# Feature-product inputs in cells of a 128-row block by a token tile, placed 0 or 32 bytes into the cell by stage, with the low parts of the input weight chunks 32 bytes into their slots

## What is computed

```
h = rms_norm(x, g)            # 256 tokens x 1024
a = h @ w_in                  # input product, 1024 -> 2 x 2816 in a feed-forward part
x = x + f(a) @ w_out          # output product, 2816 -> 1024 there, 1024 -> 1024 in a mixer
```

## Time and profile before

| | before |
|---|---|
| three executions | 2536.23, 2537.78, 2538.86 us |
| the profiled execution | 2536.61 us, its span 2534.8 us |
| TensorE's granted clock | 1.0 of full speed throughout (2.4 GHz) |
| busy: PE, PEld, DVE, ACT | 2518.7, 2223.5, 1769.4, 1395.5 us |
| share of PE in the chain that ended last | 95% |

### The profile page before, as it was taken

The page is one execution under the profiler, slowest core; times in us unless marked ns, Lnnn a source line. Parts: engine busy times, 40 slices in busy tenths (PEclk is TensorE's granted clock), DMA queues, the critical chain, the costliest instruction groups (busy, mean ns, idle before and its releaser), DMA issues.

```text
span 2534.8 us, 37208 instructions
## 1 busy us (share of the span) xinstructions
PE 2518.7 (99%) x15209; PEld 2223.5 (88%) x15209; DVE 1769.4 (70%) x2500; ACT 1395.5 (55%) x2078; POOL 150.6 (6%) x228
## 2 busy tenths in 40 slices
PE   9999999999999999999999999999999999999999
PEld 9999888998888988888888888888988888898887
DVE  7778567885775777757657775775777577567773
ACT  7766476664554555545555554554555455455553
POOL 2100011000000000000010000002010000010000
PEclk9999999999999999999999999999999999999999
DMA  7266552664665556556564655655456556563763
GB/s 224 98 178 211 173 166 84 189 194 166 208 196 197 181 162 194 189 187 197 185 221 147 204 192 187 195 187 196 153 166 201 188 180 205 184 207 125 216 189 127
DMA packets 543027, 459.47 MB, mean 181 GB/s; under 512 B 10634, under 2 KB 500058, under 8 KB 542858
## 3 DMA queue, kind: packets, MB, share of 16 engines
q1 hardware_dynamic: 537351, 441.52, 54.9%
q0 software_dynamic: 4656, 15.30, 1.7%
q10 hardware_dynamic: 851, 0.28, 0.0%
HBM read 455.97 MB, written 1.10 MB: 180 GB/s over the span
## 4 chain that ended last, share of the span: by engine, by line
PE 95%; DVE 3%; ACT 1%; DMA 1%; issue 0%; POOL 0%; DVEq 0%; POOLq 0%; ACTq 0%
PE ps L964 28%; PE ps L847 23%; PE ps L846 11%; PE ps L829 5%; PE ps L830 5%; PE ps L831 5%; PE ps L784 2%; PE ps L783 2%; PE ps L782 2%; PE ps L765 2%; PE ps L766 2%; PE ps L767 2%; PE ps L849 1%; PE ps L687 1%; DVE wlo L1956 1%; PE ps L1065 1%
## 5 line engine op out<-in xcount | busy, mean ns | idle before, releaser
L1956 DVE TENSOR_TENSOR wlo<-raw,whi 128x2048 fp32r<-128x2048 f32 (+1 forms) x419 | 956.7, 2287 | 363.2 <-ACT whi L1362 363.1
L1362 ACT ACTIVATE whi<-raw 128x2048 fp32r<-128x2048 f32 (+2 forms) x421 | 800.3, 1906 | 293.2 <-DMA raw<-in_ff_w_out 161.1
L847 PE MATMUL ps<-h,whi 128*128 128x512 f32 x2560 | 873.6, 393 | 0.0
L846 PE MATMUL ps<-h,wlo 128*128 128x256 f32 x2240 | 629.7, 281 | 0.0
L847 PEld LDWEIGHTS ps<-h,whi 128*128 128x128 f32 x2560 | 459.7, 188 | 81.5
L846 PEld LDWEIGHTS ps<-h,wlo 128*128 128x128 f32 x2240 | 421.9, 188 | 15.3
L1362 ACT ACTIVATE u<-ps 128x512 f32<-128x512 f32 x160 | 96.0, 600 | 397.4 <-PE ps L847 397.4
L964 PE MATMUL ps<-whi,hid_hi 128*128 128x512 f32 x880 | 291.3, 390 | 0.0
L964 PE MATMUL ps<-whi,hid_lo 128*128 128x512 f32 x880 | 290.7, 389 | 0.0
L964 PE MATMUL ps<-wlo,hid_hi 128*128 128x512 f32 x880 | 290.3, 389 | 0.0
L829 PE MATMUL ps<-h,whi 128*128 128x256 f32 x1024 | 288.1, 281 | 0.0
(11 more groups left out here) (337 smaller groups left out, 3285.9 us busy)
## 6 DMA issues: line engine op xcount, KB each, us to landing
raw<-in_ff_w_in SPq DMA_DIRECT2D x160, 1024.0 KB, 5.6
raw<-in_ff_w_out SPq DMA_DIRECT2D x88, 1024.0 KB, 4.8
raw<-in_ffn_w_in SPq DMA_DIRECT2D x40, 1024.0 KB, 5.6
raw<-in_a_w_qkv SPq DMA_DIRECT2D x24, 1024.0 KB, 5.0
raw<-in_ffn_w_out SPq DMA_DIRECT2D x22, 1024.0 KB, 4.8
raw<-in_w_in SPq DMA_DIRECT2D x18, 1024.0 KB, 6.2
raw<-in_ff_w_in SPq DMA_DIRECT2D x32, 512.0 KB, 4.4
raw<-in_c_w_qkv SPq DMA_DIRECT2D x12, 1024.0 KB, 5.0
```

The costliest lines, as they stand in the source:

```text
L846: e.matmul(out[:, 0:SEQ], lo, m.h[:, 0, k, :], start=False, stop=False, skip_group_check=True)
L847: ins = e.matmul(view(out, a=2), hi, m.h[:, :, k, :], start=(k == 0), stop=(k == KT - 1), skip_group_check=True)
L1362: return self.nc.scalar.activation(*a, **k)
L1956: self.e.tensor_tensor(chunk_view(m.wlo[:, slot, :], c), chunk_view(m.raw[:, slot, :], c), chunk_view(m.whi[:, slot, :], c).bitcast(F32), ...
```

## The change

The tile `h` gets a dimension more: 2 x 8 x 2 cells of 128 + 16 floats, one for a block and a token tile (576 bytes apart). A stage's input product writes and reads its 128 floats 8 floats (32 bytes) into the cell, a mixer's output product at offset 0. A stream of 256 tokens is now two rows of 128 with 64 bytes between them, one of 512 four such rows. The slots of `raw`/`wlo` get 16 floats more (8256 bytes instead of 8192), and the chunks of input products are put 8 floats in, by the DMA too; those of output products stay at offset 0, and `whi` stays as it was. The fillers around `h` go; `v_mla` moves into other tiles' unused ends. In `mix` of the second layer, ScalarE evicts the first token tile before the `split` instead of after it, waiting for that tile's reciprocal deviation alone. No instruction is added or taken away.

```diff
+H_AT = {"out": 0, "mix1": 8, "mix2": 8, "ffn1": 8, "swiglu": 8}
+PAD = 16
+LOW_IN = 8
+LOW_SWIGLU = 8
...
-        dst, src = dst_src(self.m.raw[:, c % SLOTS, :], b)
+        dst, src = dst_src(low(self.m.raw, c), b)
...
-                hi, lo = w_of(m.whi[:, c % SLOTS, :], f, k), w_of(m.wlo[:, c % SLOTS, :], f, k)
-                e.matmul(out, hi, m.h_hi[:, k, :], start=(k == 0), stop=False)
-                e.matmul(out, hi, m.h_lo[:, k, :], start=False, stop=False)
-                ins = e.matmul(out, lo, m.h_hi[:, k, :], start=False, stop=(k == KT - 1))
+                hi, lo = w_of(m.whi[:, c % SLOTS, :], f, k), w_of(low(m.wlo, c), f, k)
+                e.matmul(out, hi, self.inputs[:, 0, k, :, :], start=(k == 0), stop=False)
+                e.matmul(out, hi, self.inputs[:, 1, k, :, :], start=False, stop=False)
+                ins = e.matmul(out, lo, self.inputs[:, 0, k, :, :], start=False, stop=(k == KT - 1))
...
-                hi, lo = w_of(m.whi[:, c % SLOTS, :], f, k), w_of(m.wlo[:, c % SLOTS, :], f, k)
+                hi, lo = w_of(m.whi[:, c % SLOTS, :], f, k), w_of(low(m.wlo, c), f, k)
                 if k > 0:
-                    e.matmul(out[:, 0:SEQ], lo, m.h[:, 0, k, :], start=False, stop=False, skip_group_check=True)
-                ins = e.matmul(view(out, a=2), hi, m.h[:, :, k, :], start=(k == 0), stop=(k == KT - 1), skip_group_check=True)
+                    e.matmul(view(out[:, 0:SEQ], a=TT), lo, self.inputs[:, 0, k, :, :], start=False, stop=False, skip_group_check=True)
+                ins = e.matmul(out.rearrange("p (a t c) -> p a t c", a=2, t=TT), hi, self.inputs[:, :, k, :, :], start=(k == 0), stop=(k == KT - 1), skip_group_check=True)
...
-        self.blocks(OUT_ORDER[what], (self.m.h_hi, self.m.h_lo, 0), False)
+        self.blocks(OUT_ORDER[what], (self.m.out_hi, self.m.out_lo, 0), False)
...
-        if l > 0:
-            self.split(0, 0)
-        e.wait_ge(s.rstd, TT * self.rounds["norm"])
         if l == 0:
+            e.wait_ge(s.rstd, TT * self.rounds["norm"])
             keep(0)
             self.split(0, 0)
             keep(1)
         else:
             for t in range(TT):
+                e.wait_ge(s.rstd, TT * (self.rounds["norm"] - 1) + t + 1)
                 self.evict_head(t, proj, C_CQ, HEAD_WIDTH, ACT.Copy)
+                if t == 0:
+                    self.split(0, 0)
...
+def low_places():
+
+    out = []
+    for stage in PLAN:
+        n, rows = chunks_of(stage), 4 if stage[0] in ("mix1", "mix2") else FT // 2
+        out += [LOW_SWIGLU if stage[0] == "swiglu" else LOW_IN] * (n - rows) + [0] * rows
+    return out
+
+
+def low(a, c):
+
+    return a[:, c % SLOTS, LOW_AT[c]:LOW_AT[c] + CW]
...
-            [("raw", [P, SLOTS, CW])],
-            [("wlo", [P, SLOTS, CW], F32R)])
-        sb(ctx, "in_front_of_h", [P, 8])
-        m.h = sb(ctx, "h", [P, 2, KT, SEQ], F32R)
-        sb(ctx, "behind_h", [P, 120])
-        m.h_hi, m.h_lo = m.h[:, 0, :, :], m.h[:, 1, :, :]
+            [("raw", [P, SLOTS, CW + PAD])],
+            [("wlo", [P, SLOTS, CW + PAD], F32R)])
+        m.h = sb(ctx, "h", [P, 2, KT, TT, P + PAD], F32R)
+        m.h_at = lambda stage: m.h[:, :, :, :, H_AT[stage]:H_AT[stage] + P]
+        m.out_hi, m.out_lo = (m.h_at("out")[:, i, :, :, :] for i in range(2))
```

More of the change, by code:

```diff
@@ L725, in turn_rows, with take @@
         ins.then_inc(s.rows_turned, 1)
+    def take(self, stage):
+        self.inputs = self.m.h_at(stage)
     def begin_product(self):
@@ L756, in tokens_tile @@
         c = self.c0 + b
-        whi, wlo = (a[:, c % SLOTS, :].rearrange("p (k c) -> p k c", k=KT)[:, :, 0:w] for a in (m.whi, m.wlo))
+        whi, wlo = (a.rearrange("p (k c) -> p k c", k=KT)[:, :, 0:w] for a in (m.whi[:, c % SLOTS, :], low(m.wlo, c)))
         out = m.ps[:, self.bank(b), t * 256:t * 256 + w]
@@ L772, in pair_tile @@
         c = self.c0 + b
-        whi, wlo = (a[:, c % SLOTS, 0:PAIR * w].rearrange("p (k c) -> p k c", k=PAIR) for a in (m.whi, m.wlo))
+        whi, wlo = (a[:, 0:PAIR * w].rearrange("p (k c) -> p k c", k=PAIR) for a in (m.whi[:, c % SLOTS, :], low(m.wlo, c)))
         out = m.ps[:, t, 0:w]
@@ L823, in features_chunk @@
                 between()
-            out = m.ps[:, self.bank(b), f * 256:(f + 1) * 256]
+            out = view(m.ps[:, self.bank(b), f * 256:(f + 1) * 256], a=TT)
             for k in range(KT):
@@ L999, in down @@
         self.by_group, self.what = False, kind
-        self.blocks(range(FT // 2), (self.m.hid_hi, self.m.hid_lo, 4), True)
+        hi, lo = (a.rearrange("p f (t c) -> p f t c", t=TT) for a in (self.m.hid_hi, self.m.hid_lo))
+        self.blocks(range(FT // 2), (hi, lo, 4), True)
     def out(self, what, l):
@@ L1377, in split @@
         self.at(s.landed[slot], 16 * landings(c))
-        self.act(chunk_view(m.whi[:, slot, :], c), chunk_view(m.raw[:, slot, :], c), ACT.Copy).then_inc(s.split_hi, 1)
+        self.act(chunk_view(m.whi[:, slot, :], c), chunk_view(low(m.raw, c), c), ACT.Copy).then_inc(s.split_hi, 1)
     def start(self):
@@ L2009, in rotary_angles, with turn_lo @@
         e.tensor_scalar(m.ang[:, :], m.ang0[:, :], lim, -lim, ALU.min, ALU.max).then_inc(s.angles, 1)
-    def turn_lo(self, t, gain, only=None):
+    def turn_lo(self, t, gain, stage, only=None):
         e, m, s = self.e, self.m, self.s
+        h_hi, h_lo = (m.h_at(stage)[:, i, :, :, :] for i in range(2))
         if t == 1 and only is None:
@@ L2051, in split_first @@
         self.e.wait_ge((s.first_hi, s.split_hi)[half], 1)
-        whi, wlo, raw = (chunk_view(a[:, 0, :], 0)[:, 4 * half:4 * half + 4, :] for a in (m.whi, m.wlo, m.raw))
+        whi, wlo, raw = (chunk_view(a, 0)[:, 4 * half:4 * half + 4, :] for a in (m.whi[:, 0, :], low(m.wlo, 0), low(m.raw, 0)))
         self.e.tensor_tensor(wlo, raw, whi.bitcast(F32), ALU.subtract).then_inc((s.first_lo, s.split_lo)[half], 1)
@@ L2116, in edge @@
             if after is not None:
-                self.turn_lo(1, gain)
+                self.turn_lo(1, gain, after[0])
         else:
@@ L2128, in edge @@
                 self.add_sum(1, 0)
-            self.turn_lo(0, gain)
+            self.turn_lo(0, gain, after[0])
             if scaled:
```

108 lines of the change are left out of this document (58 added, 50 removed).

## The result

The changed kernel takes 2557.73 us (median of four executions, 2556.41 to 2559.26) against 2537.31 for the kernel before (four executions by now): a ratio of 1.008 (95% interval 1.0063 to 1.0098), 20 us slower. The forecast was 2523, with 2500 to 2548 as its range, so it was wrong in sign and in range. The profiled execution has a span of 2557.2 us.

A forecast was written before the change was run, and what follows sets the result against it. PE, busy 99% of the span, was taken to bound the kernel through matmul start-to-start distances. Terms -8.4 - 3.6 - 1.3 + 0 - 1.4 = -14.7 us gave 2521.9 for the profiled execution, 2523 as median; range 2500 to 2548.

The forecast's parts named there:

- rival 3: Places repeat over 128 bytes or more, not 64: feed-forward output products +18.2 us, PE gains lost, 2555 us; chance 0.09.
- down: Output product of a feed-forward part, 2640 matmuls in all at 226.8 ns; no term in the sum, so 0.
- The wide chunks: 320 blocks: 512-wide h streams and wlo loads come to the same place; 345.5 instead of 348.8 ns a pair, -8.4 us.
- Out: Output products of mixers: h loaded from offset 0, 528 matmuls from 233.7 to 226.8 ns, -3.6 us.
- The first two chunks: First two chunks of a stage: wlo streamed from 32 beside an h load at 32, 224 matmuls, -1.3 us.
- Features at 0: Features chunks, 256-wide: one of three matmuls gets stream and load at one place; no reason for either sign, 0.
- The breaks at 0: Extra breaks in streamed rows, one more in 256 columns and two more in 512, costed at nothing.
- rival 2: Every break in a streamed row costs, up to 3.3 ns for 10752 breaks: +20.8 us, 2559; chance 0.11.
- The order on ACT: Second mixer: first token tile evicted before the split, so PE starts chunk 2 earlier, released by DVE; -1.4 us.
- DMA and splits at 0: Splits and DMAs now 32 bytes in may take longer, but slack before their use hides it: both 0.
- Rival 1: The change moves nothing on PE, places do not matter; only the ACT order gains: 2536.4 us; chance 0.18.

The follow-up runs named there:

- e1: Kernel before with the filler behind h cut, so hid and all tiles behind it start 320 bytes past a multiple of 512: 2554.36 us, ratio 1.0067.
- e7: Kernel before with the filler behind h cut to 8 floats, so hid starts 64 bytes past a multiple of 512: 2554.72 us, ratio 1.007.
- e8: Kernel before with the filler behind h cut to 56 floats, so hid starts 256 bytes past a multiple of 512: 2536.56 us, ratio 1.0.
- e12: Changed kernel with h by token tile first (tiles 8320 bytes apart), slots of 8320, low parts shifted for gated feed-forward inputs alone: 2546.35 us, ratio 1.0039.
- the f runs: f1 to f4: distances of slots, of h's pieces, or both made multiples of 256 bytes, then all tiles moved by 64: 2527.49, 2535.4, 2523.71, 2536.04 us.
- e6: Kernel before with only h moved, to a multiple of 512 bytes, so every stream and load starts at the same place: 2543.95 us, ratio 1.0025.
- e3: Changed kernel with a filler of 48 floats behind h, so hid is on a multiple of 512 bytes again: 2549.02 us, ratio 1.0047.
- e5: Kernel before with only raw and wlo moved, by 32 bytes for all chunks, slots still 8192 bytes apart: 2544.52 us, ratio 1.0029.
- f1: Changed kernel with h in a row, low parts shifted for gated feed-forward inputs alone, slots 8448 bytes apart, hid on a multiple of 256: 2527.49 us, ratio 0.996.
- e10: Changed kernel with h in a row, low parts shifted for gated feed-forward inputs alone, slots still 8256 bytes apart: 2547.89 us, ratio 1.0042.
- f3: Slots of f1 and h layout of f2 together, inputs 32 bytes in and outputs at offset 0: 2523.71 us, ratio 0.9947.
- e2: Changed kernel without the 32-byte shift of the low parts, slots 8192 bytes apart again; h's cells and the ACT order stay: 2540.53 us, ratio 1.0013.
- f2: Kernel before with the new ACT order and h by token tile first, tiles 8448 bytes apart, with all the change's breaks: 2535.4 us, ratio 0.9997.
- e4: Kernel before with only the new order on ACT at the second mixer: 2534.95 us, ratio 0.9992.
- f4: Kernel before with the new ACT order and 64 bytes of filler ahead of whi, moving all tiles together: 2536.04 us, ratio 0.9996.

## Why the prediction was wrong, step by step

**The assumption under every step** was that only the place within 64 bytes counts, and that equal places are cheap in every product. Both readings it was made from (`down` against `out`: 389 against 395) compared 0 with 32 in a kernel where everything else was a multiple of 512; they could not tell a period of 64 from any longer one, which the prediction says in rival 3 alone. By e1, e7, e8, e12 and the f runs it is 256. And e6 shows 512-wide streams that are dear at equal places.

**down, costed at 0 and not listed at all as touched**: +13.9 us. This is the step that failed: a term put at nothing for want of looking at what moved. The change moves `hid` by 320 bytes past its multiple of 512 (e1 alone: +17.4) and scatters `wlo` (e3: 6.5 us stay when `hid` is back). Rival 3 had the mechanism and the place, at a chance of 0.09; it priced `down` at +18.2 and arrived at 2555, against 2557.7. That its total is so near is in part luck: it had `down` 4.3 us too dear and nothing for the 8.5 us of the wide chunks and features. The argument that held it down, that `hi_first` at 416 costs what `h` at 32 does, does not exclude a period of 256: 416 is 160 past a multiple of 256, 160 is dear as 32 is, and two dear places look alike.

**The wide chunks, -8.4 forecast**: +4.5 measured. The size was right where only `wlo` moves: -8.1 in e5, -8.2 in f1. The reason given for it, stream and load at the same place, is not: in e6 they are at the same place too, and these streams cost 599.0 us and not 584. Why the shift of `wlo` alone pays stays open. What undid it in the changed kernel is the distance of slots and cells (8256 and 576 bytes); in e10, with such slots and h in a row 128 bytes off, they cost 594.9. **Out, -3.6**: -0.5 measured, with cells and slots all over the multiples of 64; -2.4 in f3, so the size too was a third too large. **The first two chunks, -1.3 besides the order**: -0.7.

**Features at 0**: +4.0. e2 puts 5.8 us on the cells, and f2 shows it is their places, not the breaks. **The breaks at 0** was right, and rival 2, which came out nearest in time (2559), was right by accident: its mechanism costs nothing measurable (f2: at 1 ns each the 10752 breaks would cost 10.8 us, and its interval ends 1.5 us above the kernel before). **The order on ACT, -1.4**: right (e4, e2 and the changed kernel: 0.4 us of wait are left, released by DVE as forecast). **DMA and splits at 0**: right. The splits take what they took. A DMA of a wide chunk lands 0.5 us later with the low parts 32 bytes in (also in e5; not in e2, where they are at 0). ACT waits longer for these (52.2 us in all, 35.9 before), but no wait of PE for them comes of it. The page after, answering:

```profile
L1968 DVE TENSOR_TENSOR wlo<-raw,whi 128x2048 fp32r<-128x2048 f32 (+1 forms) x419 | 956.6, 2287 | 381.9 <-ACT whi L1371 381.8
...
raw<-in_ff_w_in SPq DMA_DIRECT2D x160, 1024.0 KB, 6.1
```

**Rival 1**, that places do not matter, fell with e1: the tile that the weights are loaded from moves by 320 bytes modulo 512, and each of 2640 matmuls costs 6.6 ns more. The Trainium skill, TensorE: Matmul & The Clock Gate, section on what happens when you issue a matmul, has the next load take nothing from the running stream. The runs do not agree: what a stream and the load beside it cost together hangs on the distance of their places.

What stays open: why 256 bytes, why the price inside the period takes the values it does (in `down` and out 227 at the same place, about 233 at 32 bytes off, 232 to 234 at 64 or 128 off), why the wide chunks and features are dear where everything starts at the same place, and whether it is the load behind a stream, the one before it, or both that count. The runs measure these prices and explain none of them. Distances other than these were not tried one by one.

## What to carry to other kernels

When an edit changes the size of a tile, list every tile that is allocated behind it and every loop that reads one: here 16 floats of padding in each slot of one tile cost 14 us in a product that the change never mentions. Pad rows, slots and cells of what TensorE reads to multiples of 256 bytes, and choose offsets inside that by a run for each kind of product, since no offset was best for all of them here; a comparison of two places in the trace says what those two cost, but not the period, and a filler tile of a few floats measures it for the price of one run. If a cause explains a figure (rival 2 hit the time within 2 us), look first whether it explains the stage in which the time was lost.

## What the runs showed of the hardware

- The distance between the starts of a 512-wide float32 stream and of the weight load beside it counts modulo 256 bytes: in `down` 226.8 ns a matmul at 0 and 256, 233.5 at 320, 233.3 at 64, 232.3 at 384 (with slots 128 bytes off by turns). That is up to 3% of such a matmul at the full clock. Moving all tiles together by 64 bytes changes nothing (f4).
- A streamed row in two or four pieces costs nothing against one in one piece, as long as the pieces keep their place in 256 bytes (f2: 281, 279 and 279 ns for features, as in the kernel before).
- What is cheap depends on the neighbours. With everything at the same place (e6) 512-wide streams among 512-wide ones are cheapest (out, 390 ns against 395), 512-wide ones that alternate with 256-wide ones are dear (396 against 393), and so are the 256-wide ones of features_chunk (283 against 279). Moving `wlo` alone by 32 bytes (e5) raises all three forms of `down`, from 390, 389 and 389 to 393, 393 and 396, also the two that do not stream it.
